# Moving the buffers that TensorE reads to multiples of 256 bytes, with 4128 bytes between the chunk buffers of the split weights, in a transformer block kernel

## The chip, the cores and the metric

The kernel runs on one core of one Trainium2 chip. The metric is the device time of one execution in microseconds. Before the change it is 1143.13 us, the median of three runs that lie between 1142.49 and 1143.39 us.

## The reference, cut to what matters

One block over 256 tokens of width 2048 in float32: RMS norm, one projection to 6152 columns, half of them for four mLSTM heads and half for four differential attention heads, an output projection 2048x2048, a second norm and a SwiGLU of width 5632.

```python
def reference(x, norm1_w, w_in, ..., w_gate, w_up, w_down):
    for l in range(DEPTH):                        # DEPTH = 1
        h = rms_norm(x, norm1_w[l])
        x = x + mixer(h, l, w_in[l], ..., w_out[l])
        h = rms_norm(x, norm2_w[l])
        x = x + swiglu(h, w_gate[l], w_up[l], w_down[l])
    return x

def swiglu(h, w_gate, w_up, w_down):
    return (jax.nn.silu(h @ w_gate) * (h @ w_up)) @ w_down
```

All inputs and outputs are float32. The weights of the four big products are some 205 MB.

## The kernel before

**The products.** Every product of activations and weights is made of three matmuls. Each operand is split into a high half, which is its value rounded to the type float32r of one pass, and a low half, which is what the rounding left. For one tile of 128 rows of the contraction, 128 tokens and 512 output columns the function `chunk` (L369) issues high activations by low weights (L379), low by high (L381) and high by high (L382), all into one PSUM bank. The activations are the stationary operand: TensorE loads 128x128 elements of them (512 bytes of a partition) ahead of each matmul. The weights are the moving operand: 512 elements (2048 bytes) of a partition stream through the array in one matmul.

**The stream of weights.** The weights lie in HBM as 392 chunks of 128x1024 elements (4096 bytes of a partition) in the order in which they are used: 96 chunks of the input projection, 32 of the output projection, 176 of gate and up, 88 of the down projection. A chunk is loaded by SyncE's queue into one of four buffers of `w_raw` (L311), ScalarE rounds it into one of four buffers of `w_hi` (L646, in loops L653), VectorE subtracts and writes `w_lo` (L899), and TensorE makes 12 matmuls of it. So the stream has 4704 matmuls. Semaphores tie them: `raw_landed`, `hi_done`, `lo_done` and `chunk_used`. ScalarE may fill buffer n modulo 4 again when TensorE has used chunk n-4, and SyncE may load again when `w_lo` of chunk n-4 is made. The rest of the work is put between the chunks by hand, at chunk numbers that stand in the constants `AT_...` (L77 to L86): transposes of 128x128 by an identity matrix (L393), the gate sums (L403, L404), attention (L442, L443, L461 to L463) and mLSTM (L493 to L508).

**Where things lie.** Tensors in SBUF are placed one behind another in the order in which they are declared, each rounded up to 32 bytes. Ahead of `res` lie 16384 bytes that are kept for DMA descriptors and four constants of 32 bytes each, so `res` begins at byte 16512, which is 128 past a multiple of 256. `act_hi`, `act_lo`, `w_raw`, `w_hi` and `w_lo` have 16384 bytes each, `stage`, `scaled` and `gated` 4096 each, `ident` 512; so all of these begin 128 bytes past a multiple of 4096. `par`, `small` and the filler `line_pad` (L147) bring `y_hi`, `y_lo`, `hid_hi` and, by way of `hid_pad`, `hid_lo` to the same 128 past a multiple of 4096. A stationary slice of `act_hi`, `y_hi` or `hid_hi` begins at a multiple of 512 from its tensor's start, a moving slice of `w_hi` or `w_lo` at a multiple of 2048. Hence each of the 4704 matmuls of the stream has both operands at 128 past a multiple of 512. Three groups lie otherwise. The stationary operand `w_if_parts` of the gate sums begins at byte 187040 and moves on by 64 bytes with each of the 16 slices k, so its slices begin 160, 224, 32, 96, 160, ... past a multiple of 256, while the moving operand (`act_hi`, `act_lo`) stays at 128. `aq`, `ak`, `av`, `mq`, `mk` begin at multiples of 256. `mv`, `a_mat`, `a_turn` and `m_w` begin at 160 (`mv` has rows of 257 elements). These last groups are plain float32 matmuls, which the chip runs as two passes.

The order of the queues: SyncE's queue carries all the loads and stores but three. The loads of the start are five of `xt` (L315), four of `res` (L318) and the first eight chunks.

Of the kernel before, what the change touches and what calls it, by code (L numbers as in the profile page):

```python
# [27 lines left out]
F32 = mybir.dt.float32  # L28
F32R = mybir.dt.float32r
ALU = mybir.AluOpType  # L30
ACT = mybir.ActivationFunctionType
# [10 lines left out]
CH = 2 * NG  # L42
# [8 lines left out]
RAW = 4  # L51
SPLIT = 4
# [36 lines left out]
def hybrid_block_kernel(nc, x, x_turned, params, gate_bias, gate_w, weights, out):  # L89
    ctx = ExitStack()  # L90
    with ctx:
        def sb(name, shape, dt=F32, stack=ctx, parts=P):
            return stack.enter_context(nc.sbuf_tensor(name, [parts] + shape, dt))

        def sem(name):
            return ctx.enter_context(nc.semaphore(name))


        res = sb("res", [TT, D])
        act_hi = sb("act_hi", [KT, SEQ], F32R)  # L100
        act_lo = sb("act_lo", [KT, SEQ], F32R)
        w_raw = sb("w_raw", [RAW, CH])
        w_hi = sb("w_hi", [SPLIT, CH], F32R)
        w_lo = sb("w_lo", [SPLIT, CH], F32R)
        stage = sb("stage", [TT, NG])
        scaled = sb("scaled", [TT, NG])
        gated = sb("gated", [TT, NG])
# [36 lines left out]
        one_col = small[:, 154:155]  # L144


        sb("line_pad", [24 + 608])  # L147

        start = ExitStack()
        xt = sb("xt", [KT, SEQ], F32, start)  # L150
# [57 lines left out]
        hi_done = sem("hi_done")  # L208
# [423 lines left out]
        def _(act):  # L632
# [8 lines left out]
            def split_hi(n, slot):  # L641

                act.wait_ge(raw_landed[slot], 16 * (n // RAW + 1))
                if n >= SPLIT:
                    act.wait_ge(chunk_used, n - (SPLIT - 1))
                act.activation(w_hi[:, slot, :], w_raw[:, slot, :], ACT.Copy).then_inc(hi_done, 1)  # L646

            def split_hi_from(start, ahead, c):


                act.wait_ge(raw_landed[c % RAW], ahead * (16 // RAW) + 16 * ((start + c) // RAW + 1))
                act.wait_ge(chunk_used, ahead + (start + c - (SPLIT - 1)))
                act.activation(w_hi[:, c % SPLIT, :], w_raw[:, c % RAW, :], ACT.Copy).then_inc(hi_done, 1)  # L653

            def turned_hi(dst, j, t):

# [192 lines left out]
            for n in range(FF0):  # L849
                split_hi(n, n % SPLIT)  # L850
                small_work(n)
                if n > OUT0 + GC and (n - OUT0) % GC == LAG - 1:
                    x1_squares((n - OUT0) // GC - 1)
                if n > OUT0 + GC and (n - OUT0) % GC == 2 * LAG:
                    x1_hi((n - OUT0) // GC - 1)

            def ff_slice(i, first):
                for c in range(FF_CHUNKS):
                    split_hi_from(FF0, i * FF_CHUNKS, c)
                    if c == LAG - 1 and first:  # L860
                        x1_squares(3)
                    if c == 2 * LAG and first:
                        x1_hi(3)
                        act.wait_ge(x1_tot, 1)
                        act.activation(root, tot, ACT.Sqrt, bias=eps, scale=1.0 / D).then_inc(x1_root, 1)
                    if c == 2 * LAG and not first:
                        hidden_hi(i)
                    if c == GC + LAG - 1:
                        if first:
                            act.wait_ge(r2_ready, 1)  # L870
                        gate(i, first)
# [4 lines left out]
            for c in range(2 * SPLIT):  # L876
                split_hi(DOWN0 + c, c % SPLIT)
                if c == 2 * LAG:
                    hidden_hi(FF_SLICES)
            with act.Fori(2, 2 * KF // SPLIT) as i:  # L880
                for c in range(SPLIT):
                    split_hi_from(DOWN0, i * SPLIT, c)
# [3 lines left out]
        def _(dve):  # L886
# [9 lines left out]
            def split_lo(n, slot):  # L896

                dve.wait_ge(hi_done, n + 1)
                dve.tensor_tensor(w_lo[:, slot, :], w_raw[:, slot, :], w_hi[:, slot, :].bitcast(F32),  # L899
                                  ALU.subtract).then_inc(lo_done, 1)  # L900

            counts = {"turns": 0}
# [263 lines left out]
            for n in range(FF0):  # L1166
                if n == 0:
                    dve.wait_ge(par_landed, 16)
                    x_lo(0)
                split_lo(n, n % SPLIT)  # L1170
                small_work(n)
                free_group(n)
                if n > OUT0 + GC and (n - OUT0) % GC == LAG - 1:
                    x1_group((n - OUT0) // GC - 1)
                if n > OUT0 + GC and (n - OUT0) % GC == 2 * LAG:
                    x1_block((n - OUT0) // GC - 1)

            def ff_slice(i, first):
                for c in range(FF_CHUNKS):
                    split_lo(i * FF_CHUNKS + (FF0 + c), c % SPLIT)  # L1180
                    if first and c == LAG - 1:
                        x1_group(3)
                    if first and c == 2 * LAG:
                        x1_block(3)
                        dve.wait_ge(x1_squared, 4)
                        dve.tensor_reduce(tot, ss_x1, AX.X, ALU.add).then_inc(x1_tot, 1)
                        dve.wait_ge(x1_root, 1)
                        dve.reciprocal(r2, root).then_inc(r2_ready, 1)
                        dve.wait_ge(r2_ready, 1)
                    if not first and c == LAG - 1:  # L1190
                        hidden(i)
                    if not first and c == 2 * LAG:
                        hidden_lo(i)
# [17 lines left out]
            for c in range(2 * SPLIT):  # L1211
                split_lo(DOWN0 + c, c % SPLIT)
                if c == LAG - 1:
                    hidden(FF_SLICES)
                if c == 2 * LAG:
                    hidden_lo(FF_SLICES)
# [51 lines left out]
```

## Time and profile before

| what | value |
|---|---|
| median of three runs | 1143.13 us (1142.49 to 1143.39) |
| the profiled execution, its own time | 1142.86 us |
| its span, first to last instruction | 1141.0 us |
| mean granted TensorE clock | 0.998 of full |
| TensorE matmul busy (PE) | 1122.4 us, 98% |
| TensorE weight loads busy (PEld) | 929.1 us, 81% |
| VectorE (DVE) | 600.8 us, 53% |
| ScalarE (ACT) | 537.6 us, 47% |
| GpSimd (POOL) | 4.5 us |
| DMA queue of SyncE | 54.9% of 16 engines |

The profile is of one execution. Matmuls are pipelined and their ends are modelled: a matmul of the stream has a duration of 0.39 us in the records, but the next one starts 0.23 us after it. So the distance from start to start is the number to read, and not the duration. A few per cent of the records of matmuls can be missing. PEclk is the granted clock of TensorE as a share of 2.4 GHz.

### The profile page before, as it was taken

The numbers are of one execution on the slowest core, as the hardware profiler recorded it, in microseconds if no ns is written. First come the engines' busy times: TensorE is split into PE (matmuls) and PEld (weight loads), VectorE is DVE, ScalarE is ACT, GpSimd is POOL, SyncE is SP. The second block draws the span as 40 slices with busy tenths as digits, with TensorE's granted clock in tenths as the row PEclk, the third lists the DMA queues.
The fourth block names the chain that finished last, engine by engine and source line by source line (L and its number), as shares of the span: only waits on it lengthen the run. The fifth ranks groups of instructions, "written<-read, shape, count | busy, mean of one in ns | idle before, by whom it ended". The sixth has DMA issues, their size and how long they took to land.

```text
span 1141.0 us, 14440 instructions
## 1 busy us (share of the span) xinstructions
PE 1122.4 (98%) x5064; PEld 929.1 (81%) x5064; DVE 600.8 (53%) x685; ACT 537.6 (47%) x665; POOL 4.5 (0%) x20
## 2 busy tenths in 40 slices
PE   6999999899999999999999999999999999999998
PEld 5888887788888888888888888888888888888886
DVE  5576456664566664454554554544544544454443
ACT  7565476654554454444444434444444433333332
POOL 1000000000000000000000000000000000000000
PEclk9999999999999999999999999999999999999999
DMA  9555444554455656555555555555555555555664
GB/s 353 186 175 181 161 141 137 173 191 153 149 201 175 195 167 205 195 182 193 184 199 184 185 200 186 184 193 188 188 185 192 183 196 196 191 193 193 194 193 130
DMA packets 59651, 212.45 MB, mean 186 GB/s; under 512 B 6736, under 2 KB 6736, under 8 KB 59616
## 3 DMA queue, kind: packets, MB, share of 16 engines
q1 hardware_dynamic: 59408, 211.84, 54.9%
q8 instruction: 26, 0.43, 0.2%
q10 hardware_dynamic: 144, 0.05, 0.0%
q14 instruction: 9, 0.07, 0.0%
q0 software_dynamic: 64, 0.07, 0.0%
HBM read 209.83 MB, written 2.10 MB: 186 GB/s over the span
## 4 chain that ended last, share of the span: by engine, by line
PE 96%; DVE 2%; ACT 1%; issue 0%; DMA 0%; ACTq 0%
PE acc L379 27%; PE acc L382 27%; PE acc L381 27%; PE aux L382 3%; PE aux L381 3%; PE aux L379 3%; PE aux L393 2%; DVE w_lo L899 1%; DVE conv L1067 0%; DMA xt<-in_x_turned 0%; PE aux L443 0%; ACT w_hi L646 0%; DVE res L1209 0%; PE aux L495 0%; ACT conv L780 0%
## 5 line engine op out<-in xcount | busy, mean ns | idle before, releaser
L899 DVE TENSOR_TENSOR w_lo<-w_raw,w_hi 128x1024 fp32r<-128x1024 f32 x392 | 478.5, 1225 | 451.8 <-ACT w_hi L653 333.3
L379 PE MATMUL acc<-w_lo,act_hi 128*128 128x512 f32 x1088 | 429.2, 395 | 13.3 <-DVE w_lo L899 13.3
L653 ACT ACTIVATE w_hi<-w_raw 128x1024 fp32r<-128x1024 f32 x256 | 271.3, 1061 | 359.3 <-PE acc L382 227.1
L382 PE MATMUL acc<-w_hi,act_hi 128*128 128x512 f32 x1088 | 425.0, 391 | 0.0
L381 PE MATMUL acc<-w_hi,act_lo 128*128 128x512 f32 x1088 | 424.6, 390 | 0.0
L379 PEld LDWEIGHTS acc<-w_lo,act_hi 128*128 128x128 f32 x1088 | 205.1, 188 | 57.3 <-issue 10.7
L382 PEld LDWEIGHTS acc<-w_hi,act_hi 128*128 128x128 f32 x1088 | 204.8, 188 | 43.2
L381 PEld LDWEIGHTS acc<-w_hi,act_lo 128*128 128x128 f32 x1088 | 205.2, 189 | 41.5
L646 ACT ACTIVATE w_hi<-w_raw 128x1024 fp32r<-128x1024 f32 x136 | 141.9, 1056 | 79.3 <-PE acc L382 70.3
L379 PE MATMUL acc<-w_lo,hid_hi 128*128 128x512 f32 x176 | 68.6, 390 | 0.0
L382 PE MATMUL aux<-w_hi,hid_hi 128*128 128x512 f32 x176 | 68.5, 389 | 0.0
L379 PE MATMUL aux<-w_lo,hid_hi 128*128 128x512 f32 x176 | 68.5, 389 | 0.0
L382 PE MATMUL acc<-w_hi,hid_hi 128*128 128x512 f32 x176 | 68.5, 389 | 0.0
L381 PE MATMUL aux<-w_hi,hid_lo 128*128 128x512 f32 x176 | 68.5, 389 | 0.0
L381 PE MATMUL acc<-w_hi,hid_lo 128*128 128x512 f32 x176 | 68.5, 389 | 0.0
L379 PE MATMUL acc<-w_lo,y_hi 128*128 128x512 f32 x128 | 50.2, 392 | 0.0
L382 PE MATMUL acc<-w_hi,y_hi 128*128 128x512 f32 x128 | 49.9, 390 | 0.0
L381 PE MATMUL acc<-w_hi,y_lo 128*128 128x512 f32 x128 | 49.8, 389 | 0.0
L381 PEld LDWEIGHTS aux<-w_hi,hid_lo 128*128 128x128 f32 x176 | 33.0, 188 | 6.9
L381 PEld LDWEIGHTS acc<-w_hi,hid_lo 128*128 128x128 f32 x176 | 33.0, 188 | 6.9
L379 PEld LDWEIGHTS acc<-w_lo,hid_hi 128*128 128x128 f32 x176 | 33.0, 188 | 6.9
L379 PEld LDWEIGHTS aux<-w_lo,hid_hi 128*128 128x128 f32 x176 | 33.0, 188 | 6.9
(191 smaller groups left out, 533.6 us busy)
## 6 DMA issues: line engine op xcount, KB each, us to landing
w_raw<-in_weights SPq DMA_DIRECT2D x392, 512.0 KB, 4.0
res<-in_x SPq DMA_DIRECT2D x4, 512.0 KB, 10.1
out<-res SPq DMA_DIRECT2D x8, 256.0 KB, 3.8
xt<-in_x_turned SPq DMA_DIRECT2D x3, 512.0 KB, 8.7
xt<-in_x_turned SPq DMA_DIRECT2D x2, 256.0 KB, 4.8
w_if<-in_gate_w POOLq DMA_DIRECT2D x1, 64.0 KB, 6.1
par<-in_params ACTq DMA_DIRECT2D x1, 47.0 KB, 4.2
bias_if<-in_gate_bias POOLq DMA_DIRECT2D x1, 0.0 KB, 5.6
```

What stands on the lines that cost most here:

```text
L379: pe.matmul(bank[:], hi[:, k, tok], w_lo[:, slot, cols], start=first and kk == 0, stop=False)
L381: pe.matmul(bank[:], lo[:, k, tok], w_hi[:, slot, cols], start=False, stop=False)
L382: mm = pe.matmul(bank[:], hi[:, k, tok], w_hi[:, slot, cols], start=False, stop=last and kk == len(kts) - 1)
L393: mm = pe.transpose(banks[t][:, P * b:P * (b + 1)], src[:, t, P * b:P * (b + 1)], ident[:])
L646: act.activation(w_hi[:, slot, :], w_raw[:, slot, :], ACT.Copy).then_inc(hi_done, 1)
L653: act.activation(w_hi[:, c % SPLIT, :], w_raw[:, c % RAW, :], ACT.Copy).then_inc(hi_done, 1)
L899: dve.tensor_tensor(w_lo[:, slot, :], w_raw[:, slot, :], w_hi[:, slot, :].bitcast(F32), ALU.subtract).then_inc(lo_done, 1)
```

## The change

Filler tensors move what lies behind them. A filler of 128 bytes ahead of `res` moves `res`, `act_hi`, `act_lo`, `w_raw` and `w_hi` from 128 past a multiple of 256 to a multiple of 256. The rows of `w_hi` and `w_lo` grow by 8 elements, to 4128 bytes, of which the last 32 are not used; a filler of 128 bytes behind each of them brings what follows to a multiple of 256 again. So chunk buffers 0, 1, 2 and 3 of each half begin 0, 32, 64 and 96 bytes past a multiple of 256. `line_pad` shrinks by 512 bytes, so that everything behind it moves by 128 bytes: `y_hi`, `y_lo`, `hid_hi` and `hid_lo` to multiples of 256, `mv`, `a_mat`, `a_turn` and `m_w` from 160 to 32, the slices of `w_if_parts` to 32, 96, 160, 224, and `aq`, `ak`, `av`, `mq` and `mk` from 0 to 128. No instruction, wait or transfer is added or removed; three access patterns name the first 1024 elements of a row in place of the whole row.

```diff
+        sb("front_pad", [32])
         res = sb("res", [TT, D])
         act_hi = sb("act_hi", [KT, SEQ], F32R)
         act_lo = sb("act_lo", [KT, SEQ], F32R)
         w_raw = sb("w_raw", [RAW, CH])
-        w_hi = sb("w_hi", [SPLIT, CH], F32R)
-        w_lo = sb("w_lo", [SPLIT, CH], F32R)
+        w_hi = sb("w_hi", [SPLIT, CH + 8], F32R)
+        sb("hi_pad", [32])
+        w_lo = sb("w_lo", [SPLIT, CH + 8], F32R)
+        sb("lo_pad", [32])
...
-        sb("line_pad", [24 + 608])
+        sb("line_pad", [24 + 608 - 128])
...
-                act.activation(w_hi[:, slot, :], w_raw[:, slot, :], ACT.Copy).then_inc(hi_done, 1)
+                act.activation(w_hi[:, slot, 0:CH], w_raw[:, slot, :], ACT.Copy).then_inc(hi_done, 1)
...
-                act.activation(w_hi[:, c % SPLIT, :], w_raw[:, c % RAW, :], ACT.Copy).then_inc(hi_done, 1)
+                act.activation(w_hi[:, c % SPLIT, 0:CH], w_raw[:, c % RAW, :], ACT.Copy).then_inc(hi_done, 1)
...
-                dve.tensor_tensor(w_lo[:, slot, :], w_raw[:, slot, :], w_hi[:, slot, :].bitcast(F32),
+                dve.tensor_tensor(w_lo[:, slot, 0:CH], w_raw[:, slot, :], w_hi[:, slot, 0:CH].bitcast(F32),
                                   ALU.subtract).then_inc(lo_done, 1)
```

## Rows read from the trace of the kernel before

**Rows 1.** The page's first part and TensorE's row in 40 slices

```profile
PE 1122.4 (98%) x5064; PEld 929.1 (81%) x5064; DVE 600.8 (53%) x685; ACT 537.6 (47%) x665; POOL 4.5 (0%) x20
PE   6999999899999999999999999999999999999998
```

**Rows 2.** The chain that ended last, by engine

```profile
PE 96%; DVE 2%; ACT 1%; issue 0%; DMA 0%; ACTq 0%
```

**Rows 3.** The chain in order of time: the first load, two turns of a gate-and-up slice

```profile
0.75 4.04 DMA xt<-in_x_turned
...
640.58 0.87 PE aux L393 x8
...
685.02 0.87 PE aux L393 x8
```

**Rows 4.** What TensorE waited for: us in total, times, longest us

```profile
PE acc L379 <- DVE w_lo L899: 13.3, 4, 9.4
```

**Rows 5.** Down projection, matmul starts (start us, duration us) of one chunk

```profile
1000.17 0.39 PE L382 MATMUL aux<-w_hi,hid_hi 128*128 128x512 f32 x1
...
1001.53 0.39 PE L382 MATMUL acc<-w_hi,hid_hi 128*128 128x512 f32 x1
...
1002.89 0.39 PE L382 MATMUL aux<-w_hi,hid_hi 128*128 128x512 f32 x1
```

**Rows 6.** Plain float32 passes of attention, two to a row, in the timeline

```profile
144.38 0.60 PE L461 MATMUL aux<-av,a_turn 128*128 128x256 f32 x2
144.81 0.59 PE L462 MATMUL aux<-av,a_turn 128*128 128x256 f32 x2
145.24 0.59 PE L463 MATMUL aux<-av,a_turn 128*128 128x256 f32 x2
145.67 0.38 PE L442 MATMUL aux<-ak,aq 128*128 128x128 f32 x2
```

**Rows 7.** A window: its us, PE busy (matmuls), granted clock, DMA share, GB/s

```profile
220.90:224.10 3.20, 3.20 (x9) 0.50 0.67 188
```

**Rows 8.** The stream's matmul starts in that window, timeline

```profile
221.07 0.63 PE L382 MATMUL acc<-w_hi,act_hi 128*128 128x512 f32 x1
...
223.63 0.63 PE L382 MATMUL acc<-w_hi,act_hi 128*128 128x512 f32 x1
```

**Rows 9.** Gate sums, matmul starts of slices k = 0, 2, 3, 10, 11 and 15

```profile
40.98 0.28 PE L403 MATMUL aux<-act_hi,w_if_parts 128*128 128x256 f32 x1
...
41.58 0.28 PE L404 MATMUL aux<-act_lo,w_if_parts 128*128 128x256 f32 x1
41.70 0.28 PE L403 MATMUL aux<-act_hi,w_if_parts 128*128 128x256 f32 x1
41.81 0.28 PE L404 MATMUL aux<-act_lo,w_if_parts 128*128 128x256 f32 x1
...
43.49 0.28 PE L404 MATMUL aux<-act_lo,w_if_parts 128*128 128x256 f32 x1
...
43.72 0.28 PE L404 MATMUL aux<-act_lo,w_if_parts 128*128 128x256 f32 x1
...
44.67 0.28 PE L404 MATMUL aux<-act_lo,w_if_parts 128*128 128x256 f32 x1
```

**Rows 10.** Groups by line: busy us, mean ns of one, idle before and releaser

```profile
L899 DVE TENSOR_TENSOR w_lo<-w_raw,w_hi 128x1024 fp32r<-128x1024 f32 x392 | 478.5, 1225 | 451.8 <-ACT w_hi L653 333.3 <-ACT w_hi L646 117.8
L653 ACT ACTIVATE w_hi<-w_raw 128x1024 fp32r<-128x1024 f32 x256 | 271.3, 1061 | 359.3 <-PE acc L382 227.1 <-PE aux L382 132.2
L922 DVE TENSOR_TENSOR act_lo<-scaled,act_hi 128x512 fp32r<-128x512 f32 x8 | 5.2, 689 | 0.4
L658 ACT ACTIVATE act_hi<-scaled 128x512 fp32r<-128x512 f32 x8 | 4.9, 633 | 11.4 <-DVE scaled L912 11.4
```

**Rows 11.** DMA issues: KB each, median us from issue to landing

```profile
w_raw<-in_weights SPq DMA_DIRECT2D x392, 512.0 KB, 4.0
```

## The prediction

> **What bounds the kernel now.** The first part of the page says who is busy: TensorE 98% of the span, VectorE 53%, ScalarE 47% [rows 1]. The chain that ended last is TensorE for 96% [rows 2], and all it ever waited for in the stream is 13.3 us, 9.4 of them before its first matmul [rows 4]. So neither the loads nor the two splitting engines set the pace; the matmuls do. Busy time can't say how well they run, since they overlap. Hence the timeline, from start to start. A chunk of the down projection takes 1002.89 - 1000.17 = 2.72 us for 12 matmuls, 226.7 ns each [rows 5]. Gate and up keep the same pace: from one turn of a slice to the next 44.44 us pass [rows 3], of which 192 x 0.2267 = 43.5 are matmuls and 0.9 the eight transposes. With 4704 matmuls the stream is 4704 x 0.2267 = 1066 us of the 1141.0 us span. Nothing but this distance can move the time much.
>
> 512 columns at 2.4 GHz are 213.3 ns, so each matmul has an excess of 13.3 ns, 32 columns' worth. Three stretches tell what it depends on. Where the granted clock is 0.50, which is 1.2 GHz [rows 7], six matmuls take 223.63 - 221.07 = 2.56 us, 426.7 ns each: exactly 512 columns at 1.2 GHz, no excess [rows 8]. So it is not a fixed number of array cycles between two matmuls, but something that falls behind only when the array takes a 4-byte element of each partition every 0.42 ns: the supply of operands from SBUF. Second, plain float32 passes, 256 columns at half that rate, follow each other in (145.67 - 144.38) / 6 = 215.0 ns [rows 6], an excess of 1.7 ns, with operands at 0 and 160 past a multiple of 256 alike. Third, the gate sums are float32r with 256 columns, and their stationary operand wanders through the addresses: (44.67 - 40.98) / 31 = 119.0 ns, less 106.7 makes an excess of 12.4 ns [rows 9]. It hardly shrinks with half the columns, so it comes once per matmul. It isn't quite uniform either: from L404 to L404, two matmuls, slices 3 and 11 take 0.23 us (41.58 to 41.81, 43.49 to 43.72), the others 0.24. These two lie 512 bytes apart.
>
> **The change part by part.** No instruction is added or removed, so no queue, wait or order changes. (a) **Slots 1 to 3 of the split weights** now start 32, 64 and 96 bytes off their old phase against the stationary operand. They carry three quarters of the stream, 3528 matmuls. The trace has no float32r matmul with a moving operand off its usual phase; it has the gate sums, where the stationary one is off. Bounds: above, the present 13.3 ns plus the piece that a moved start may cost (rival 3); below, 1.7 ns as in plain passes. I take the gate sums' mean, 12.4, as the nearest row, since it averages over many phases: 3528 x 0.9 = 3.2 us less. At the best pair of slices (0.23 / 2 = 115 ns, excess 8.3, uncertain by 5 for the rounding) it would be 3528 x 5.0 = 17.6 us. (b) **Slot 0 and the base at a multiple of 256.** In slot 0 both operands move by the same 128 bytes. Their phase against each other mod 256 stays; I take nothing, with rival 2 for the case that the start itself counts. (c) **Plain passes and transposes**: `aq`, `ak`, `av`, `mq`, `mk` go from 0 to 128, `mv` and the like from 160 to 32. Rows 6 show 215.0 ns with either kind: nothing; if they lost their cover of half rate the page's 5064 matmuls less the stream and the gate sums are some 330 passes, at 10 ns 3 us. (d) **ScalarE and VectorE** write rows that start at other addresses. Their 1024-element forms take 1061 and 1225 ns, the 512-element forms 633 and 689 [rows 10], which is 0.84 and 1.05 ns an element with no extra term, and both engines idle between chunks until TensorE or each other is done. Nothing; their cover is that idle time (359 us for ScalarE's loop), and only a slowdown of over half a microsecond a chunk would reach the path. (e) **Loads** land in `w_raw` and `xt` at multiples of 256. In the stream they land 4.0 us after issue [rows 11] and TensorE never waits for them. Only the first `xt` load, 4.04 us [rows 3], is on the path; between nothing and a ninth of it (a block less of nine) I take 0.1 us less. The Trainium skill, page DMA: Bandwidth & Descriptors, section How a descriptor splits into AXI transactions, states that a transfer that starts off 256 bytes costs an extra transaction; the trace has no aligned load to compare.
>
> The sum: 1142.86 (the profiled execution: 1141.0 span and 1.86 around it) - 3.2 - 0.1 = 1139.6. The median of the runs shown is 0.27 above the profiled execution: 1139.8.
>
> What row and page say of the excess differs. Measured are 226.7 ns [rows 5]. The Trainium skill, TensorE: Matmul & The Clock Gate, section Back-to-back issue gap, gives N/2.4 + 2.5 ns, 215.8 here; the trace disagrees by 10.9 ns, and by that page the estimate for a kernel without the excess would be 51 us less.
>
> **Rivals.**
> 1. **Nothing moves** (0.29). The excess belongs to float32r at 2.4 GHz wherever the operands lie: 12.4 against 13.3 at quite other stationary phases [rows 9] speaks for it, the uneven slices against it. Time 1143.1. The Trainium skill, SBUF — State Buffer, section Who interferes with whom, says that TensorE's two read ports are independent and never wait; by this rule the result would be this rival's, and the trace only fits if the excess is no conflict at all.
> 2. **The start of the moving read counts** (0.12). Reads come in blocks of 256 bytes: 128 bytes off are 32 elements, 32 columns at 2.4 GHz, 13.3 ns, exactly the excess measured, and hidden at 1.2 GHz and at half rate. Then slots 0 to 3 would have 0, 8, 16 and 24 columns: 1.7 (the floor of rows 6), 3.3, 6.7 and 10.0 ns, mean 5.4; 4704 x 7.9 = 37 us less, 1106. Against it: the gate sums' moving operand is at 128 too and shows 12.4, below 13.3. Beside it, **a conflict of the two reads that the new phases end** (0.07): down to 1.7 ns in all slots, 4704 x 11.6 = 55 us less, 1089.
> 3. **Slower** (0.22). A moving read that starts at an odd multiple of 32 bytes touches one more piece of 64. Slots 1 and 3, half of the stream, pay 32 bytes, 8 columns, 3.3 ns: 2352 x 3.3 = 7.8 us, 1151. It decides once the mean distance is above 227.2 ns (0.5 ns x 4704 = 2.3 us). For it: today every moving read begins on a multiple of 128 and nothing shows what others cost in float32r. Against it: stationary starts at 32 mod 64 in the gate sums cost nothing. The Trainium skill, SBUF — State Buffer, Specifications, has lines of 16 bytes; by that rule no start here would cost more than before.
>
> **How the numbers follow.** My forecast, a small gain by phase, is the rest: 0.30, its own range 1126 to 1141. A measurement of this kernel can tell about 0.2%, 2.3 us, from no change. Faster by more: 0.30 + 0.12 + 0.07 = 0.49; same 0.29; slower 0.22. The range runs from 1104, which holds rival 2's blocks, to 1151, the slower rival's price; outside lie the full removal and the tails.
>
> **What would show it.** Right: starts in a chunk of the down projection some 225 to 226.4 ns apart on the mean, slots unequal (chunks of slot 0 at 2.72 us, one of the others at 2.70 or less), the same busy times of ScalarE and VectorE, gate sums near 119 ns. Rival 1: 2.72 us in every chunk. Rival 2: chunk lengths that rise with the slot, 2.58, 2.60, 2.64, 2.68 us. Rival 3: slots 1 and 3 at 2.76. The forecast is wrong if all four slots are equal at another value than 2.72: then the base address counts and not the spacing. If the pace quickens much, waits for `w_lo` on TensorE between chunks 16 and 96, where small work fills the other engines, are late next. A stall there that halves the clock for 3.2 us as in rows 7 costs about 1.6 us.

## The result and the profile after

The changed kernel takes 1164.67 us (median of four runs, 1164.14 to 1165.09) against 1142.81 us of the kernel before (1142.09 to 1143.39): a ratio of 1.0189, 95% interval 1.0177 to 1.0201. It is slower by 1.9%. The profiled execution has a span of 1163.3 us against 1141.0, so 22.3 us have to be found. Line numbers behind the declarations are three higher than before.

The first part of the page (busy us, share, instructions), from the engines' totals:

```profile
PE 1144.8 (98%) x5064; PEld 929.4 (80%) x5064; DVE 601.3 (52%) x685; ACT 538.2 (46%) x665; POOL 4.5 (0%) x20
```

TensorE's busy time has grown by 22.4 us [rows 1], all the others stand still. The chain in order of time (start us, us) has the groups of eight transposes ("turns") of gate and up in it, which divide the kernel:

```profile
0.75 4.25 DMA xt<-in_x_turned
...
425.10 0.87 PE aux L396 x8
...
606.62 0.87 PE aux L396 x8
...
652.00 0.87 PE aux L396 x8
...
924.27 0.87 PE aux L396 x8
...
1156.85 0.69 DVE res L1212
```

The same view of the kernel before:

```profile
418.44 0.87 PE aux L393 x8
...
907.16 0.87 PE aux L393 x8
1134.55 2.73 DVE res L1209 x4
```

Up to the first of these turns 425.10 - 418.44 = 6.7 us are lost, over the eleven slices behind it (924.27 - 425.10) - (907.16 - 418.44) = 10.5 us, one slice taking 45.38 us in place of 44.44 [rows 3], and behind the last turn, in the down projection, (1156.85 - 924.27) - (1134.55 - 907.16) = 5.2 us. The sum is 22.3 us, spread over the whole stream of weights. The timeline of the down projection (start us, duration us) shows how. Five chunk starts, of buffers 0, 1, 2, 3 and 0:

```profile
1047.43 0.39 PE L382 MATMUL acc<-w_lo,hid_hi 128*128 128x512 f32 x1
...
1050.19 0.40 PE L382 MATMUL acc<-w_lo,hid_hi 128*128 128x512 f32 x1
...
1052.99 0.40 PE L382 MATMUL acc<-w_lo,hid_hi 128*128 128x512 f32 x1
...
1055.75 0.40 PE L382 MATMUL acc<-w_lo,hid_hi 128*128 128x512 f32 x1
...
1058.56 0.39 PE L382 MATMUL acc<-w_lo,hid_hi 128*128 128x512 f32 x1
```

The chunks take 2.76, 2.80, 2.76 and 2.81 us in place of 2.72 [rows 5]; averaged over the ten chunks of each buffer at the end of the timeline that is 230.1, 233.6, 229.9 and 234.2 ns from start to start. Four chunks are 11.13 us, 231.9 ns a matmul, 5.2 more than the 226.7 of before. No wait has come: TensorE waits for `w_lo` as long as before [rows 4], as the list of waits says (us, times, longest):

```profile
PE acc L382 <- DVE w_lo L902: 13.3, 4, 9.6
```

ScalarE and VectorE write the moved rows at the old speed [rows 10] (groups by line: busy us, mean ns | idle, releaser), and a chunk lands hardly sooner, after 3.8 us in place of 4.0 [rows 11]:

```profile
L902 DVE TENSOR_TENSOR w_lo<-w_raw,w_hi 128x1024 fp32r<-128x1024 f32 x392 | 478.8, 1225 | 468.1 <-ACT w_hi L656 346.7 <-ACT w_hi L649 120.6
L656 ACT ACTIVATE w_hi<-w_raw 128x1024 fp32r<-128x1024 f32 x256 | 271.4, 1061 | 372.6 <-PE acc L385 235.4 <-PE aux L385 137.2
```

And the stretch from which the prediction took its price, the gate sums, keeps its pace: the timeline has 31 distances in 45.49 - 41.80 = 3.69 us, 119.0 ns each, as in [rows 9]. Both its operands moved by the same 128 bytes, so their distance is what it was:

```profile
41.80 0.28 PE L406 MATMUL aux<-act_hi,w_if_parts 128*128 128x256 f32 x1
...
45.49 0.28 PE L407 MATMUL aux<-act_lo,w_if_parts 128*128 128x256 f32 x1
```

### The profile page after: what moved, and what is told of

Same layout as the page of the kernel before. It is cut to its first block, busy times and chain, and to the rows that moved or that the text cites. A ratio compares the mean times of both kernels' runs of the same rounds, so it can differ in the third digit from the quotient of the medians.

```text
span 1163.3 us, 14440 instructions
## 1 busy us (share of the span) xinstructions
PE 1144.8 (98%) x5064; PEld 929.4 (80%) x5064; DVE 601.3 (52%) x685; ACT 538.2 (46%) x665; POOL 4.5 (0%) x20
## 4 chain that ended last, share of the span: by engine, by line
PE 96%; DVE 2%; ACT 1%; issue 0%; DMA 0%; ACTq 0%
PE acc L382 27%; PE acc L385 27%; PE acc L384 27%; PE aux L384 3%; PE aux L385 3%; PE aux L382 3%; PE aux L396 2%; DVE w_lo L902 1%; DVE conv L1070 0%; DMA xt<-in_x_turned 0%; ACT w_hi L649 0%; PE aux L446 0%; DVE res L1212 0%; PE aux L498 0%; PE aux L407 0%
## 5 line engine op out<-in xcount | busy, mean ns | idle before, releaser
L382 PE MATMUL acc<-w_lo,act_hi 128*128 128x512 f32 x1088 | 433.5, 398 | 13.3 <-DVE w_lo L902 13.3
L385 PE MATMUL acc<-w_hi,act_hi 128*128 128x512 f32 x1088 | 430.1, 395 | 0.0
L384 PE MATMUL acc<-w_hi,act_lo 128*128 128x512 f32 x1088 | 429.7, 395 | 0.0
L385 PEld LDWEIGHTS acc<-w_hi,hid_hi 128*128 128x128 f32 x176 | 33.1, 188 | 7.9
```

What stands on the lines that cost most here:

```text
L382: pe.matmul(bank[:], hi[:, k, tok], w_lo[:, slot, cols], start=first and kk == 0, stop=False)
L384: pe.matmul(bank[:], lo[:, k, tok], w_hi[:, slot, cols], start=False, stop=False)
L385: mm = pe.matmul(bank[:], hi[:, k, tok], w_hi[:, slot, cols], start=False, stop=last and kk == len(kts) - 1)
```

## The experiments

Below, "phase" is the address of the moving operand less that of the stationary one, modulo 256. Before the change it is 0 for all 4704 matmuls. A matmul out of phase has a phase other than 0, and the pace of 226.7 ns is called in step. Where fillers change the sum of the sizes, `line_pad` takes it up, so that what lies behind it stays unless the text says otherwise. Paces are distances from start to start in the timeline, in the down projection mostly over four chunks, 48 matmuls.

**The two halves of the change, each alone.** The first moves every buffer by 128 bytes and keeps the rows of 4096 bytes:

```diff
+        sb("front_pad", [32])
         res = sb("res", [TT, D])
```

> Half of the change alone: 128 bytes of filler ahead of res and 96 bytes... in all 128 bytes for every buffer, rows of w_hi and w_lo left at 4096 bytes. Every buffer begins at a multiple of 256 and all have the same distances as before. Theory P (phase: the distance between the moving and the stationary operand's address counts, not where either starts): 226.7 ns from start to start in every slot, 1143 us. Theory S (start: an operand's own address against a fixed block counts): the 230.1 ns of slot 0 of the changed kernel in all slots, 4704 x 3.4 ns = 16 us more, 1159 us.

Measured: 1143.04 us, ratio 1.0001 (0.999 to 1.0012). Four chunks of the down projection take 10.88 us, 226.7 ns a matmul, the old pace:

```profile
1027.52 0.39 PE L380 MATMUL acc<-w_lo,hid_hi 128*128 128x512 f32 x1
...
1038.40 0.39 PE L380 MATMUL acc<-w_lo,hid_hi 128*128 128x512 f32 x1
```

The second keeps the base and takes the rows of 4128 bytes:

```diff
-        w_hi = sb("w_hi", [SPLIT, CH], F32R)
-        w_lo = sb("w_lo", [SPLIT, CH], F32R)
+        w_hi = sb("w_hi", [SPLIT, CH + 8], F32R)
+        sb("hi_pad", [32])
+        w_lo = sb("w_lo", [SPLIT, CH + 8], F32R)
+        sb("lo_pad", [32])
```

> The other half alone: rows of 4128 bytes and the two fillers behind w_hi and w_lo, all else at 128 past a multiple of 256 as before. Distances between operands are those of the changed kernel. Theory P: the changed kernel's four chunk lengths, 230.1, 233.6, 229.9, 234.2 ns a matmul, 1164.7 us. Theory S: slot 0 as before at 226.7 ns, slots 1 and 3 dearer by what an odd multiple of 32 costs (about 4 ns), some 1152 us.

Measured: 1164.87 us, ratio 1.019 (1.016 to 1.022), and the changed kernel's four chunk lengths to the hundredth:

```profile
1047.05 0.39 PE L381 MATMUL acc<-w_lo,hid_hi 128*128 128x512 f32 x1
...
1049.81 0.40 PE L381 MATMUL acc<-w_lo,hid_hi 128*128 128x512 f32 x1
...
1052.61 0.40 PE L381 MATMUL acc<-w_lo,hid_hi 128*128 128x512 f32 x1
...
1055.37 0.40 PE L381 MATMUL acc<-w_lo,hid_hi 128*128 128x512 f32 x1
...
1058.18 0.39 PE L381 MATMUL acc<-w_lo,hid_hi 128*128 128x512 f32 x1
```

So the multiples of 256 do nothing, and the spacing does all of it.

**Start or phase.** Everything 32 bytes further (`front_pad` of 8 elements):

> All buffers 32 bytes further than before, rows of 4096 bytes, same distances between operands. Theory P: 226.7 ns, 1143 us. Theory S, by which starts at odd multiples of 32 bytes cost: at least the 3.5 ns of slot 1 against slot 0 on every matmul, 1160 us or more.

Measured: 1142.73 us, ratio 0.9997 (0.9986 to 1.0009), 226.7 ns in all buffers. A start at an odd multiple of 32 costs nothing as long as both operands make the move. Then `w_lo` alone 256 bytes further:

```diff
+        sb("hi_pad", [64])
         w_lo = sb("w_lo", [SPLIT, CH], F32R)
```

> As before, but w_lo (and stage to par behind it) 256 bytes further; rows of 4096 bytes. Of the stream only the high-by-low matmuls of L379 change their distance to the stationary operand, by 256 bytes. In slot 0 of the changed kernel this is the only distance that differs from before. Theory P with a period of over 256 bytes: 230.1 ns on the mean as there, 1159 us. Theory S, or theory P with a period of 256 or less: 226.7 ns, 1143 us.

Measured: 1142.53 us, ratio 0.9999 (0.9988 to 1.001), 226.7 ns. And the change's own form with 256 bytes in place of 32:

```diff
-        w_hi = sb("w_hi", [SPLIT, CH], F32R)
-        w_lo = sb("w_lo", [SPLIT, CH], F32R)
+        w_hi = sb("w_hi", [SPLIT, CH + 64], F32R)
+        w_lo = sb("w_lo", [SPLIT, CH + 64], F32R)
```

> The change's own form with another size: rows of w_hi and w_lo 4352 bytes apart, 256 more than before in place of 32, all else as before. The phase modulo 256 is the same in the four slots. Theories C and J: 226.7 ns in every slot, 1143 us. A theory by which the four slots must lie at multiples of 4096 (or two access patterns with gaps are slower by themselves): 230 ns or more.

Measured: 1143.01 us, ratio 1.0 (0.9988 to 1.0011). Rows with gaps are not slower in themselves, and whole 256 bytes don't count. What is left is the phase modulo 256.

**A phase held constant.** Three runs leave the weights in step and move the stationary operands alone, each stage by its own amount:

```diff
+        sb("act_pad", [32])
         act_hi = sb("act_hi", [KT, SEQ], F32R)
         act_lo = sb("act_lo", [KT, SEQ], F32R)
+        sb("raw_pad", [32])
         w_raw = sb("w_raw", [RAW, CH])
...
+        sb("hid_front", [48], F32, ff)
         hid_hi = sb("hid_hi", [KF, SEQ], F32R, ff)
```

> Rows of 4096 bytes; the stationary operands alone are moved against the weights: act_hi and act_lo by 128 bytes, y_hi and y_lo by 96, hid_hi and hid_lo by 32. So each stage has one constant phase (distance of stationary to moving operand, modulo 256). Theory C (each phase has its own cost): hid by 32 is 231 to 234 ns from start to start in the down projection, act by 128 some other constant value above or below 226.7. Theory J (only the jump of the phase from chunk to chunk costs, a constant phase locks again): 226.7 ns in all three stages, 1143 us. Theory B (there is a better phase than 0): one of the stages is below 226 ns.

> As the run before, with act by 64 bytes, y by 192, hid by 224. A stationary operand 224 further is a moving operand 32 further, as in slot 1 of the changed kernel, and 192 is its slot 2. Theory C: down projection at slot 1's 233.6 ns, output projection at slot 2's 229.9 ns, gate and up something between. Theory J: 226.7 ns in all. Theory B: one below 226 ns.

> As the two runs before, with act by 160 bytes, y by 128, hid by 96. A stationary operand 160 further is slot 3 of the changed kernel. Theory C: the input projection and gate and up at slot 3's 234.2 ns, 1142.9 + 272 x 12 x 7.5 ns = 24 us more from these alone, the output and the down projection like the same phases of the first of these runs. Theory J: 226.7 ns in all, 1143 us. Theory B: one below 226 ns.

Measured: 1169.61, 1170.90 and 1172.89 us, ratios 1.0235 (1.0191 to 1.0279), 1.0246 (1.0202 to 1.029) and 1.0264 (1.022 to 1.0308). In the first, four chunks of the down projection take 11.20 us, 233.3 ns (stationary operand 32 further); in the second, eight chunks of gate and up take 22.40 us, 233.3 ns (64 further):

```profile
1051.67 0.40 PE L382 MATMUL acc<-w_lo,hid_hi 128*128 128x512 f32 x1
...
1062.87 0.40 PE L382 MATMUL acc<-w_lo,hid_hi 128*128 128x512 f32 x1
```

```profile
575.53 0.39 PE L382 MATMUL acc<-w_lo,act_hi 128*128 128x512 f32 x1
...
597.93 0.39 PE L382 MATMUL acc<-w_lo,act_hi 128*128 128x512 f32 x1
```

No stage comes back to 226.7 ns, so theory J, by which only the jump costs, falls. In the other stages of the three runs it is read in the same way (in the output projection as the mean of its distances). The first run gives phases 128 (gate and up), 160 and 224, the second 192, 64 and 32, the third 96, 128 and 160. Together:

| phase | 0 | 32 | 64 | 96 | 128 | 160 | 192 | 224 |
|---|---|---|---|---|---|---|---|---|
| ns | 226.7 | 233.3 | 228.9 | 233.3 | 232.6 | 234.3 | 233.3 | 233.3 |

The value at 128 is a mean: in gate and up of the first run four chunks take 11.16 us (232.4 ns) in most slices and 11.20 us (233.3 ns) in others. So a phase need not have one pace only.

These runs also move the gate sums' operands against each other, and their pace does follow. Before and after the change their phases are 32, 96, 160 and 224 in turn, never 0. In the third run they are 0, 64, 128 and 192, and the 31 distances take 3.62 us, 116.8 ns each in place of 119.0:

```profile
41.79 0.28 PE L406 MATMUL aux<-act_hi,w_if_parts 128*128 128x256 f32 x1
...
45.41 0.28 PE L407 MATMUL aux<-act_lo,w_if_parts 128*128 128x256 f32 x1
```

**Between chunks.** The changed kernel's slots have the phases 0, 32, 64 and 96. By the table they would take 226.7, 233.3, 228.9 and 233.3 ns, but slot 0 takes 230.1. The next run gives buffer 3 alone a phase, through `off(slot)`, 8 elements for buffer 3 and 0 for the others, in rows of 4352 bytes:

```diff
-                        cols = slice(NG * (kk * width + j), NG * (kk * width + j + 1))
+                        cols = slice(off(slot) + NG * (kk * width + j), off(slot) + NG * (kk * width + j + 1))
```

> Chunk buffers 4352 bytes apart, and in buffer 3 alone w_hi and w_lo begin 32 bytes later. Buffers 0, 1 and 2 have phase 0 to the stationary operand, buffer 3 a moving operand 32 bytes further. In the changed kernel slot 0 has phase 0 too and yet takes 230.1 ns a matmul. Theory R (the reads carry a lag over from one matmul to the next, and need some matmuls to fall into step again after a phase with conflicts): slot 0, which follows slot 3, at 230 ns, slots 1 and 2 at 226.7, slot 3 at 233. Rival (phase 0 itself is not what slot 0's cost hangs on, the two halves' distance or the 4128-byte row is): slots 0, 1 and 2 all at 226.7 or all at 230.

Measured: 1154.37 us, ratio 1.01 (1.0071 to 1.013). Chunk starts and, in the first chunk, the ninth matmul:

```profile
1038.26 0.40 PE L382 MATMUL acc<-w_lo,hid_hi 128*128 128x512 f32 x1
...
1040.11 0.39 PE L385 MATMUL aux<-w_hi,hid_hi 128*128 128x512 f32 x1
...
1041.02 0.39 PE L382 MATMUL acc<-w_lo,hid_hi 128*128 128x512 f32 x1
...
1043.74 0.39 PE L382 MATMUL acc<-w_lo,hid_hi 128*128 128x512 f32 x1
...
1046.46 0.40 PE L382 MATMUL acc<-w_lo,hid_hi 128*128 128x512 f32 x1
...
1049.26 0.40 PE L382 MATMUL acc<-w_lo,hid_hi 128*128 128x512 f32 x1
```

Slot 0 takes 2.76 us, slots 1 and 2 2.72, slot 3 2.80. In slot 0 the first eight matmuls take 1.85 us, 231 ns each, the last four 0.91 us, 227.5. The slow pace outlasts the chunk that causes it by some seven matmuls, and that is slot 0's extra in the changed kernel. The kernel before has such a tail too, at phase 0 throughout, where transposes have broken the stream. In the first chunk behind a turn of gate and up nine distances take 2.08 us, 231 ns each, and the next nine 2.04 us, 226.7:

```profile
463.80 0.39 PE L381 MATMUL acc<-w_hi,act_lo 128*128 128x512 f32 x1
...
465.88 0.39 PE L381 MATMUL acc<-w_hi,act_lo 128*128 128x512 f32 x1
...
467.92 0.39 PE L381 MATMUL acc<-w_hi,act_lo 128*128 128x512 f32 x1
```

So the tail is not peculiar to a change of phase; a break leaves one as well.

`w_lo` alone 32 bytes off (`hi_pad` of 8 elements, `lo_pad` of 56) puts every third matmul into another phase:

> Rows of 4096 bytes, w_hi at phase 0 and w_lo 32 bytes further, so of each three matmuls one has another phase, in every chunk alike. Theory R (a lag from a conflict takes some seven matmuls to pass, as in slot 0 of the run with slot 3 alone): the pace never falls into step, above the mean of a third, (226.7 x 2 + 233.6) / 3 = 229.0, some 231 to 234 ns, 1163 us or more. Rival (each matmul pays for its own phase alone): 229.0 ns, 1154 us.

Measured: 1164.13 us, ratio 1.0184 (1.0155 to 1.0214). Four chunks take 11.12 us, 231.7 ns, above the 229.0 of matmuls that each pay for themselves:

```profile
1045.98 0.39 PE L381 MATMUL acc<-w_lo,hid_hi 128*128 128x512 f32 x1
...
1057.10 0.39 PE L381 MATMUL acc<-w_lo,hid_hi 128*128 128x512 f32 x1
```

**Finer phases.** The slots get a constant `off` of 4, then of 2 elements; `y` and `hid` are moved as the expectations say.

> Every chunk buffer of w_hi and w_lo begins 16 bytes later against act_hi and act_lo; y is moved by 32 bytes and hid by 64, so the moving operand lies 16 bytes beyond the stationary one in gate and up, 16 before it in the output projection, 48 before it in the down projection. Theory C with a block of 16 bytes or less: each of these is a phase with conflicts, 229 to 234 ns. Theory C with a block of 32 bytes or more: 16 beyond is like 0, 226.7 ns. Theory B (a phase better than 0 lies between the multiples of 32): one below 226 ns.

> As the run before with 8 bytes in place of 16 (moving operand 8 bytes beyond the stationary one in the input projection, gate and up and the down projection, 24 before it in the output projection). Theory C with a block of 16 bytes or more that is read as a whole: near 226.7 ns, at most a few columns for a start inside a block. Theory C with blocks of 8 bytes or less: 229 ns or more. Theory B: below 226 ns.

Measured: 1168.41 us, ratio 1.0223 (1.0194 to 1.0253), and 1172.53 us, ratio 1.0259 (1.023 to 1.0289). 16 bytes beyond take 231.7 ns in gate and up, 48 before 234.7 in the down projection, 16 before 236.6 in the output projection, the slowest pace of all, and 8 beyond 233.3 in gate and up and in the down projection: a phase near 0 is no better than one far off. In the first of the two, the down projection:

```profile
1049.01 0.40 PE L383 MATMUL acc<-w_lo,hid_hi 128*128 128x512 f32 x1
...
1060.28 0.40 PE L383 MATMUL acc<-w_lo,hid_hi 128*128 128x512 f32 x1
```

With `off` of 7 elements and `act` and `y` 32 bytes further the phase is -4 and 28:

> The moving operand 4 bytes before the stationary one in all stages but the down projection, 28 bytes beyond it there. Theory C with exact equality wanted: 229 to 235 ns in all stages. Theory C with a block of 8 bytes or more that is fetched as a whole: 226.7 in some of them. Theory B (a better phase than 0): below 226 ns.

Measured: 1142.12 us, ratio 0.9995 (0.9984 to 1.0006), 226.7 ns in every stage: as good as 0 and not better. In the down projection (phase 28) four chunks take 10.88 us:

```profile
1026.96 0.39 PE L385 MATMUL acc<-w_lo,hid_hi 128*128 128x512 f32 x1
...
1037.84 0.39 PE L385 MATMUL acc<-w_lo,hid_hi 128*128 128x512 f32 x1
```

Two runs asked what is special about it. The changed kernel with its moving operands at element 7 of each row:

```diff
-                        cols = slice(NG * (kk * width + j), NG * (kk * width + j + 1))
+                        cols = slice(7 + NG * (kk * width + j), 7 + NG * (kk * width + j + 1))
```

> The changed kernel with w_hi and w_lo written and read from element 7 of their 4128-byte rows on, so that the moving operands start 28, 60, 92 and 124 bytes past the stationary one's phase, at odd multiples of 4. Theory O (a moving operand that starts at an odd 4-byte word leads to the steady 226.7 ns whatever the stationary one's address): 226.7 in all four slots, 1143 us. Rival (the distance counts and only some distances, such as 28, are as good as 0): slot 0 near 227 to 230, slots 1 to 3 at 229 to 235, some 1160 us.

Measured: 1152.06 us, ratio 1.0077 (1.006 to 1.0094), between the two theories:

```profile
1035.93 0.39 PE L382 MATMUL acc<-w_lo,hid_hi 128*128 128x512 f32 x1
...
1038.65 0.39 PE L382 MATMUL acc<-w_lo,hid_hi 128*128 128x512 f32 x1
...
1041.38 0.39 PE L382 MATMUL acc<-w_lo,hid_hi 128*128 128x512 f32 x1
...
1044.16 0.39 PE L382 MATMUL acc<-w_lo,hid_hi 128*128 128x512 f32 x1
...
1046.92 0.39 PE L382 MATMUL acc<-w_lo,hid_hi 128*128 128x512 f32 x1
```

Phases 28 and 60 take 2.72 and 2.73 us, 92 and 124 take 2.78 and 2.76. So neither does an odd word free the moving operand of the phase (theory O), nor is 28 alone the exception. Slot 0 is back at its pace at once behind the slower slot 3, so a tail doesn't always follow. Then `act` 4 bytes and `hid` 36 bytes further, against moving operands that start where they did:

```diff
-        act_hi = sb("act_hi", [KT, SEQ], F32R)
+        act_hi_t = sb("act_hi", [KT * SEQ + 64], F32R)
+        act_hi = act_hi_t[:, 1:1 + KT * SEQ].rearrange("p (k s) -> p k s", k=KT)
```

> As before, but act_hi and act_lo 4 bytes further and hid_hi and hid_lo 36 bytes further, against moving operands where they were; y as before. Theory O: only the moving operand's start counts for this, so the stationary one's odd word is a phase like others: 229 to 235 ns in gate and up and in the down projection. Rival (any odd distance between the two is as good): 226.7 in both, 1143 us. If the 13.3 ns left at 226.7 come from both reads keeping to the same 8-byte words, one of the stages is below 226 ns.

Measured: 1166.65 us, ratio 1.0211 (1.0191 to 1.0232), gate and up 232.4 ns at phase -4, the down projection 233.3 at -36. The run with phases -4 and 28 had 226.7 at the same -4 with the odd word on the moving side. So the distance is not all; in the runs that moved buffers by multiples of 32 it was.

**How much the stationary operand reads.** Two runs cut its columns from 128 to 64 and to 8, leaving out the products of the tokens behind them in all but the first and last matmul of an accumulation:

```diff
-                            pe.matmul(bank[:], lo[:, k, tok], w_hi[:, slot, cols], start=False, stop=False)
+                            pe.matmul(bank[0:64, :], lo[:, k, half], w_hi[:, slot, cols], start=False, stop=False)
```

> As before, but all matmuls of the stream except the first and the last of each accumulation load 64 stationary columns in place of 128, so that for half of the tokens most of the products are left out. Phase 0 everywhere. Theory L (the excess of 13.3 ns at phase 0 is the reading of the stationary operand in the way of the moving one, in proportion to its bytes): the excess halves, about 220 ns from start to start, some 31 us less than before. Theory I (the excess belongs to every float32r matmul of 512 columns, however much is loaded): 226.7 ns, 1143 us.

> As before, but all matmuls of the stream except the first and the last of each accumulation load 8 stationary columns in place of 128, so that the products of most tokens are left out. Theory L (the excess comes from reading the stationary operand beside the moving one): with 32 bytes to read in place of 512 nothing is left to collide, about 215 to 217 ns from start to start, some 50 us less. Theory I (the excess is every float32r matmul's own): 226.7 ns, as before, or the 230 of the run with 64 columns.

Measured: 1155.73 us, ratio 1.0112 (1.008 to 1.0145), 230.0 ns; and 1159.36 us, ratio 1.0142 (1.0113 to 1.0172), 231.1 ns in the down projection:

```profile
1042.58 0.39 PE L383 MATMUL acc<-w_lo,hid_hi 128*8 128x512 f32 x1
...
1053.67 0.39 PE L383 MATMUL acc<-w_lo,hid_hi 128*8 128x512 f32 x1
```

Theory L falls: with less to load no stretch comes near 220 or 216 ns, so the 13.3 ns are not a toll by the byte. But neither is a shorter read slower in itself. In the input projection of the run with 8 columns, whole stretches are in step, four chunks in 10.88 us:

```profile
78.72 0.39 PE L383 MATMUL acc<-w_lo,act_hi 128*8 128x512 f32 x1
...
89.60 0.39 PE L383 MATMUL acc<-w_lo,act_hi 128*8 128x512 f32 x1
```

Other chunks of the same stage take 2.77 us, 231 ns a matmul, with the same forms at the same phase. So with 8 columns the stream has two steady paces, and which one it falls into after a break hangs on more than address and length; with 128 columns at phase 0 every tail ended at 226.7. These two runs also write fewer rows of PSUM, which nothing here separates from the shorter read. A third run keeps the number of columns and takes every second token (`tok = slice(t, SEQ, 2)`), so that the tokens' products come out in another order. The matmuls of t = 1, half of them, thereby start 4 bytes further, at phase -4:

> As before, but the stationary operand takes every second token in place of 128 neighbours (tokens come out permuted against the rest of the kernel), so each load walks 1024 bytes in the time in which it walked 512. act at phase 0, y with the stationary operand 64 bytes further, hid 128 bytes further. Theory L, where the two streams meet because the moving one overtakes the stationary one: a new pace in every stage, and a different one in each. Theory I: 226.7 ns at act's phase 0, as the operand's addresses but not its length have changed.

Measured: 1169.87 us, ratio 1.0234 (1.0205 to 1.0264); 22.40 us for eight chunks of gate and up, 233.3 ns at phases 0 and -4 by turns, and 231.5 in the down projection, where the stationary operand is another 128 bytes further:

```profile
576.00 0.39 PE L381 MATMUL acc<-w_lo,act_hi 128*128 128x512 f32 x1
...
598.40 0.39 PE L381 MATMUL acc<-w_lo,act_hi 128*128 128x512 f32 x1
```

Whether the step or the 4 bytes did it is not shown: 4 bytes alone, on all matmuls, gave 232.4 ns in gate and up. What is shown is that the start of the stationary read against the moving one changes the pace, and that the pace also depends on what ran before.

## Why the prediction was wrong

The forecast was 1139.8 us and faster by a little; measured are 1164.67, outside the range and on the other side. What it said of the bound holds: the matmul distance is all that moved, and it moved in the whole stream.

**The step that failed is (a), the price of slots 1 to 3**, taken as the gate sums' mean of 12.4 ns excess "as the nearest row, since it averages over many phases". The static runs put the excess at phases 32, 64 and 96 at 233.3, 228.9 and 233.3 less 213.3, 20.0, 15.6 and 20.0 ns, where (a) had 12.4 and, as its upper bound, 13.3 and a piece of 3.3. Mean over the four slots: 3.9 ns above the 226.7; 4704 of them are 18 us. The gate sums were read wrongly. Their excess "hardly shrinks with half the columns, so it comes once per matmul" set 256 columns at phases 32, 96, 160 and 224 beside 512 columns at phase 0. At those same four phases 512 columns have an excess of 20.0, 20.0, 21.0 and 20.0 ns by the table, where the gate sums have 12.4. So the excess is not the same per matmul for both lengths, and the 12.4 ns held a price for the phase: with phases 0, 64, 128 and 192 it is 10.1 ns (116.8 less 106.7). For the same reason they are no evidence for rival 1 or against rival 3, whose "stationary starts at 32 mod 64 in the gate sums cost nothing" had nothing to compare with. Before the change the trace held no 512-column float32r matmul off phase 0, so the bound above should have been open by far more than one piece.

**The second term was missing**: slot 0's phase is unchanged, as (b) says, but it pays 3.4 ns for what slot 3 left behind. Over the four slots the carry-over is 231.9 - 230.6 = 1.3 ns, some 6 us. The runs with slot 3 alone and with `w_lo` alone show it. The two terms add to 24 us against 22.3 measured; in the input projection, where small work breaks the stream and has left tails before the change too, the distances grew by some 4.3 ns only.

The rest of the parts stood. (b) Base at multiples of 256: nothing, 1.0001. Whatever a block of 256 bytes might do at the start of a read (rival 2), it does not. (c): plain passes of 256 columns take 215 to 219 ns before and after. (The section on the kernel before puts `mv` at 160; added up from the declarations it begins 128 bytes past a multiple of 256 and goes to 0. Its matmuls are plain passes too.) (d): the means of VectorE and of ScalarE's loop are the same to the nanosecond. (e): no gain; the first `xt` load took 4.25 us where it had taken 4.04. A chunk's median landing time fell from 4.0 to 3.8 us, but with `w_raw` at 128 past a multiple of 256, where it was before, the runs have medians from 3.3 to 4.2 us, so no effect of the address shows. By the Trainium skill, DMA: Bandwidth & Descriptors, section How a descriptor splits into AXI transactions, a transfer that starts at a multiple of 256 needs a transaction less; no run here shows what that is worth.

**Rival 3** had the sign at a chance of 0.22, with the right slots dearer, but neither mechanism nor size: it priced odd multiples of 32 at 3.3 ns and slots 0 and 2 at nothing. With all buffers at odd multiples of 32 the pace is 226.7. **Rival 1** does not hold: moving the stationary operands alone by 32 bytes cost 233.3 - 226.7 = 6.6 ns a matmul in the down projection. By the Trainium skill, SBUF — State Buffer, section Who interferes with whom, TensorE's two read ports are independent and it never waits. By that rule this move would have cost nothing; the runs disagree, though they don't show what waits for what. That the excess is "hidden at 1.2 GHz and at half rate", the sign that the supply of operands is involved, agrees with all this, but it was read only as something that could be taken away. The same rows allow as well that it could grow.

What stays open is the mechanism: why multiples of 256 are in step, why -4 and 28, 60 with the odd word on the moving side are as good, and why 8 stationary columns run at 226.7 ns in some stretches and 231 in others. No phase tried was below 226.7 ns, so whether the 13.3 ns can be had is open too. No version beat the kernel before.

## What to carry to other kernels

Where float32r matmuls of 512 columns follow each other with a new stationary operand each, as here, keep all stationary and moving slices of the stream at the same address modulo 256. Shifting all of them together by 32 or 128 bytes was free, but spacing buffers by a little "to spread them" cost 1.9% here. A stretch of other shape is no price for such an edit, least of all where it differs in two things at once, as the gate sums did in columns and in phase. One matmul distance of the very form, off its usual address, is worth more. And a slow pace can outlast its cause by several instructions, so a mixture of phases can cost more than its mean.

## What the runs showed that was not expected

The pace of the stream takes sharp values: 226.7 ns (544 columns' time) in step, 233.3 (560) at four of the seven other multiples of 32, with a pattern that repeats over a few matmuls. It depends on the start of the stationary read against the moving one, and on the past. After a break or a chunk out of phase, 128 columns at phase 0 come back to 226.7 ns within ten matmuls; with 8 columns some breaks leave the stream at 231 ns. The gate sums with 256 columns feel the phase too, 116.8 against 119.0 ns. Plain float32 passes of 256 columns take 215 to 219 ns at every address that the runs gave them.
